# Sample attention of a hybrid decoder step: score matmuls by halves of the keys, rope part in eight tiles of the array

## The reference

```python
def _mla_scores(q_lat, q_rope, lat, krope):
    s = jnp.einsum('bhqc,bkc->bhqk', q_lat, lat) + jnp.einsum('bhqr,bkr->bhqk', q_rope, krope)
    return s.astype(jnp.float32) * MLA_SCALE

def _softmax_accumulate(carry, s, vals):
    m, l, acc = carry
    m_new = jnp.maximum(m, jnp.max(s, axis=-1))
    corr = jnp.exp(m - m_new)
    p = jnp.exp(s - m_new[..., None])
    l_new = l * corr + jnp.sum(p, axis=-1)
    acc_new = acc * corr[..., None] + jnp.einsum('bhqk,bkc->bhqc', p, vals.astype(jnp.float32))
    return (m_new, l_new, acc_new)

    def page_step(carry, pt):          # pt: one page (128 keys) of each sequence
        lat = lat_pool[e, pt]
        kr = rope_pool[e, pt]
        s = _mla_scores(q_lat, q_rope, lat, kr)
        return _softmax_accumulate(carry, s, lat), None
```

## Time and profile before

| | |
|---|---|
| time of three runs, median | 1405.76 us (1404.13 to 1409.06) |
| the profiled execution | 1405.4 us |
| its span | 1403.5 us |
| TensorE busy in the span | 1377.5 us, 98% |
| VectorE, ScalarE, GpSimd busy | 803.4, 582.3, 113.3 us |
| granted clock of TensorE, mean | 0.996 of full speed |
| sample attention, from its first score matmul to step 0 of the output projection | 531.7 to 607.3 us |

### The profile page before, as it was taken

How to read it: one execution, slowest core, us unless ns; L and a number is a source line. 1 busy time by engine, 2 the same in 40 slices (tenths; PEclk the granted TensorE clock), 3 DMA queues, 4 the chain that set the end, 5 groups by cost and what they waited for, 6 DMA issues and landing times.

```text
span 1403.5 us, 24497 instructions
## 1 busy us (share of the span) xinstructions
PE 1377.5 (98%) x9830; PEld 1228.1 (88%) x9830; DVE 803.4 (57%) x1509; ACT 582.3 (41%) x1044; POOL 113.3 (8%) x213
## 2 busy tenths in 40 slices
PE   9999999999999999999999999999999999999996
PEld 9988999767667666689998888999999999999996
DVE  4486843174575665655886344324445659545676
ACT  4169522146556565533553233214553125212343
POOL 1000000000000305700002000010000010000000
PEclk9999999999999999999999999999999999999998
DMA  6211032220001127855556211124334030114562
GB/s 213 63 30 46 31 123 90 84 92 14 1 1 44 33 71 218 239 178 164 187 194 235 74 62 31 61 62 70 67 61 114 31 106 31 47 64 149 169 213 104
DMA packets 59298, 135.75 MB, mean 97 GB/s; under 512 B 9001, under 2 KB 37898, under 8 KB 58418
## 3 DMA queue, kind: packets, MB, share of 16 engines
q1 hardware_dynamic: 48882, 112.45, 24.4%
q0 software_dynamic: 10160, 21.56, 6.5%
q10 hardware_dynamic: 144, 0.18, 0.0%
HBM read 120.65 MB, written 13.50 MB: 96 GB/s over the span
## 4 chain that ended last, share of the span: by engine, by line
PE 86%; DVE 6%; SPq 3%; issue 2%; ACT 2%; DMA 0%; DVEq 0%; ACTq 0%
PE ps L553 14%; PE ps L555 14%; PE ps L554 14%; PE ps L682 5%; PE ps L684 5%; PE ps L683 5%; PE ps L1094 3%; PE ps L1106 2%; PE ps L1135 2%; SPq L2766 2%; PE ps L1264 2%; PE ps L3089 1%; PE ps L566 1%; PE ps L3098 1%; PE ps L3093 1%
## 5 line engine op out<-in xcount | busy, mean ns | idle before, releaser
L553 PE MATMUL ps<-x_hi,w_hi 128*128 128x352 f32 x1288 | 425.6, 330 | 0.0
L555 PE MATMUL ps<-x_hi,w_lo 128*128 128x352 f32 x1288 | 414.7, 322 | 0.0
L554 PE MATMUL ps<-x_lo,w_hi 128*128 128x352 f32 x1288 | 414.0, 321 | 0.0
L553 PEld LDWEIGHTS ps<-x_hi,w_hi 128*128 128x128 f32 x1288 | 242.3, 188 | 10.0 <-issue 9.5
L554 PEld LDWEIGHTS ps<-x_lo,w_hi 128*128 128x128 f32 x1288 | 243.1, 189 | 1.3 <-issue 1.0
L555 PEld LDWEIGHTS ps<-x_hi,w_lo 128*128 128x128 f32 x1288 | 242.2, 188 | 0.0
L495 ACT ACTIVATE w_hi<-w_raw 128x1024 fp32r<-128x1024 f32 (+1 forms) x105 | 121.2, 1154 | 246.9 <-PE ps L555 136.3
L501 DVE TENSOR_TENSOR w_lo<-w_raw,w_hi 128x1024 fp32r<-128x1024 f32 (+1 forms) x105 | 141.1, 1344 | 63.5 <-ACT w_hi L495 63.0
L682 PE MATMUL ps<-mx_hi,w_hi 128*128 128x352 f32 x480 | 157.7, 328 | 0.3 <-issue 0.2
L684 PE MATMUL ps<-mx_hi,w_lo 128*128 128x352 f32 x480 | 154.1, 321 | 0.0
L683 PE MATMUL ps<-mx_lo,w_hi 128*128 128x352 f32 x480 | 153.9, 321 | 0.0
(11 more groups left out here) (490 smaller groups left out, 1950.5 us busy)
## 6 DMA issues: line engine op xcount, KB each, us to landing
w_raw<-in_w_out SPq DMA_DIRECT2D x48, 640.0 KB, 3.9
w_raw<-in_w_in SPq DMA_DIRECT2D x57, 512.0 KB, 3.6
page<-in_cache_mla SPq DMA_DIRECT2D x128, 128.0 KB, 2.5
kvs<-in_mem_cache SPq DMA_DIRECT2D x16, 512.0 KB, 5.2
x_res<-in_xT SPq DMA_DIRECT2D x24, 176.0 KB, 2.4
x<-x_next POOLq DMA_DIRECT2D x3, 1408.0 KB, 7.6
x_res<-x SPq DMA_DIRECT2D x24, 176.0 KB, 2.3
w_mem<-in_w_mem SPq DMA_DIRECT2D x2, 2048.0 KB, 10.4
```

The lines of the kernel that those rows point to most:

```text
L553: pe.matmul(out, w_hi[:, (u + 1) % 2, kk], x_hi[:, k, chunk(c)], start=(k == 0), stop=False)
L554: pe.matmul(out, w_hi[:, (u + 1) % 2, kk], x_lo[:, k, chunk(c)], start=False, stop=False)
L555: mm = pe.matmul(out, w_lo[:, (u + 1) % 2, kk], x_hi[:, k, chunk(c)], start=False, stop=(k == KX - 1))
```

## The change

1. The scores of a round lie in two banks, 0 and 1: the first half of the 512 keys (`pair` 0, 256 keys) in bank 0 and the second half (`pair` 1) in bank 1. Even rounds use columns 0 to 255 of both banks, and odd rounds columns 256 to 511. Before, a round had one bank.
2. The latent part has 16 matmuls over 256 keys in place of 8 over 512.
3. The rope part has 8 matmuls over 256 keys in place of 4 over 512. They stand in eight different tiles of 32 by 32: sequence j keeps its column strip, and the row strip is `2 * (j // 2) + pair`. The rope keys are loaded to match: two sequences share a row strip, side by side in columns. The number and size of the loads stay.
4. The maximum and the exponential read the two halves as one operand with two pieces of 256.
5. `scores(5)`, the short round of group 1, moves from before the turn of round 6 to behind `transposes(4)`.
6. The steps of layer 0's output projection use bank `(n + 2) % 6`, so that the first of them leave banks 0 and 1 alone while round 9 is read. `BANK_FREE` follows: tile (31, 0) waits for step 22 in place of 18, (31, 1) for step 23 in place of 19, (31, 2) for 18 in place of 20, and tile 32 for steps 19, 20, 21 in place of 21, 22, 23.

The core of the diff:

```diff
+        def rope_rows(j, pair):
+            r = 32 * (2 * (j // 2) + pair)
+            return slice(r, r + 32)
+        def rope_cols(j):
+            return PAIR_COLS * (j % 2)
...
                 for k in range(2):
+                    for pair in range(2):
+                        for j in range(4):
+                            pe.matmul(ps[32 * j:32 * j + 32, pair, a:a + PAIR_COLS], rows_of(qs[:, k], g, j),
+                                      latT[:, j, k, PAIR_COLS * pair:PAIR_COLS * pair + PAIR_COLS],
+                                      start=(k == 0), stop=False, skip_group_check=True)
+                for pair in range(2):
                     for j in range(4):
-                        pe.matmul(ps[32 * j:32 * j + 32, e % 2, :], rows_of(qs[:, k], g, j), latT[:, j, k, :],
-                                  start=(k == 0), stop=False, skip_group_check=True)
-                for j in range(4):
-                    rr = slice(32 * j, 32 * j + 32)
-                    mm = pe.matmul(ps[rr, e % 2, :], rows_of(qsr[rr], g, j), ropeT[real(e) % 3][rr, :], start=False, stop=True,
-                                   skip_group_check=True)
+                        rr, cc = rope_rows(j, pair), rope_cols(j)
+                        mm = pe.matmul(ps[32 * j:32 * j + 32, pair, a:a + PAIR_COLS], rows_of(qsr[rr], g, j),
+                                       ropeT[real(e) % 3][rr, cc:cc + PAIR_COLS], start=False, stop=True,
+                                       skip_group_check=True)
...
-                    v.then(dve.tensor_reduce(col(2), bank(e % 2), AX_X, ALU.max))
+                    v.then(dve.tensor_reduce(col(2), pairs_of(e), AX_XY, ALU.max))
...
-            out = bank(n % 6, n=CH)
+            out = bank(step_bank(l, n), n=CH)
```

More of the change, by code:

```diff
@@ L27 @@
 AX_X = mybir.AxisListType.X
+AX_XY = mybir.AxisListType.XY
 P = 128
@@ L588, in build @@
             k for k in SLOTS_IN0 + SLOTS_IN1 if TILES[k[0]].kind in SIGMOIDS)}
-        BANK_FREE = {(31, 0): ZI[(0, *STEPS[18])], (31, 1): ZI[(0, *STEPS[19])], (31, 2): ZI[(0, *STEPS[20])],
-                     (32, 0): ZI[(0, *STEPS[21])], (32, 1): ZI[(0, *STEPS[22])], (32, 2): ZI[(0, *STEPS[23])]}
+        BANK_FREE = {(31, 0): ZI[(0, *STEPS[22])], (31, 1): ZI[(0, *STEPS[23])], (31, 2): ZI[(0, *STEPS[18])],
+                     (32, 0): ZI[(0, *STEPS[19])], (32, 1): ZI[(0, *STEPS[20])], (32, 2): ZI[(0, *STEPS[21])]}
         BANK_FREE.update({(33, c): ZI[(31, c)] for c in range(NCH)})
@@ L664, in sp_residual, with step_bank @@
             sp.dma_start(x_res[:, n % 2, :], src).then_inc(xr_in[n % 2], 16)
+        def step_bank(l, n):
+            return (n + (2 if l == 0 else 0)) % 6
         def pe_step(pe, l, n):
@@ L690, in dve_step @@
             dve.wait_ge(xr_in[n % 2], 16 * (12 * l + n // 2 + 1))
-            dve.scalar_tensor_tensor(res[:, t, chunk(c)], x_res[:, n % 2, :], ALPHA, bank(n % 6, n=CH),
+            dve.scalar_tensor_tensor(res[:, t, chunk(c)], x_res[:, n % 2, :], ALPHA, bank(step_bank(l, n), n=CH),
                                      ALU.mult, ALU.add).then_inc(z_free, 1)
@@ L1751, in col, with pairs_of @@
             return stat[:, c:c + 1]
+        PAIR_COLS = 2 * P
+        def pairs_of(e):
+            return ps[:, 0:2, PAIR_COLS * (e % 2):PAIR_COLS * (e % 2) + PAIR_COLS]
+        def rope_rows(j, pair):
[3 more added lines that the diff above has]
+            return PAIR_COLS * (j % 2)
         UNIT_BANKS = (2, 3, 6, 7)
@@ L1795, in scores @@
                     pe.wait_ge(ss_p, e - 1)
+                a = PAIR_COLS * (e % 2)
                 if i < 0:
@@ L1798, in scores @@
                         for j in range(4):
-                            out = ps[32 * j:32 * j + 32, e % 2, 0:SM]
+                            out = ps[32 * j:32 * j + 32, 0, a:a + SM]
                             if k < 2:
@@ L1886, in rest @@
                     nxt = e + 1 if e != 4 else 6
+                    turn(nxt, range(1 if e == 0 else 0, 6))
+                    transposes(e)
                     if e == 4:
                         scores(5)
-                    turn(nxt, range(1 if e == 0 else 0, 6))
-                    transposes(e)
                     turn(nxt, range(6, 8))
@@ L1925, in exps @@
                                                 bias=col(COL_NB + e % 2), scale=MLA_SCALE))
-                out = sp_self[:, :] if i < 0 else sp_p[:, e % 2, :]
-                act.activation(out, ps[:, e % 2, 0:out.shape[1]], ACT.Exp, bias=col(COL_NB + e % 2),
+                if i < 0:
+                    out, src = sp_self[:, :], pairs_of(e)[:, 0, 0:SM]
+                else:
+                    out, src = sp_p[:, e % 2, :].rearrange("p (b c) -> p b c", b=2), pairs_of(e)
+                act.activation(out, src, ACT.Exp, bias=col(COL_NB + e % 2),
                                scale=MLA_SCALE, accum_out=col(COL_S + e % 2)).then_inc(ss_p, 1)
@@ L1988, in maxima @@
                 if i < 0:
-                    s = ps[:, e % 2, 0:SM]
+                    s = pairs_of(e)[:, 0, 0:SM]
                     v.then(dve.tensor_tensor(s, s, selfmask[:, g, :], ALU.add))
@@ L2850, in _ @@
                     for q in range(4):
-                        gp.dma_start(ropeT[r % 3][32 * j:32 * j + 32, q * P:q * P + P],
+                        c = rope_cols(j) + (q % 2) * P
+                        gp.dma_start(ropeT[r % 3][rope_rows(j, q // 2), c:c + P],
                                      x["cache_rope"][bass.ds(four[q], 1), :, :].rearrange(
```

## The result

The changed kernel took 1408.38 us (median of 9 runs, 1405.53 to 1411.76) beside 1406.06 us for the kernel before on the same chip (9 runs). The ratio is 1.0022 [1.0013, 1.003]. Forecast were 1405.0 us and a range up to 1407.5. So the time went the other way than forecast, and lies above the range. The profiled execution is one of the faster ones: 1405.95 us, with a span of 1404.4 us against 1403.5 before. A second look at the same kernel (experiment 2) had a span of 1408.4.

What follows compares the result with a forecast made beforehand. TensorE was taken as the bound, except between 548 and 600 us, where SyncE's page loads pace it. Two savings of 0.40 us off the 1405.76 median gave 1405.0 us; range 1403.4 to 1406.4, 8 in 10 1402.6 to 1407.5.

Steps and rivals of the forecast that it cites:

- Rope part: Rope matmuls of a round's scores: eight tiles run together, 0.57 us instead of 1.00, saving 0.43.
- Two tiles at a time: Rival, slower: rope matmuls run in four sets, 1.85 us a round, giving 1407.5 us in all; chance 0.06.
- Latent part: Latent matmuls of a round's scores: 32 records of 256 columns cost 0.03 us more than the 1.83 before.
- A round: TensorE's scores of one round with pages: 0.43 saved less 0.03 lost, 0.40 us, in eight rounds.
- Start of the run of loads: First round's scores release SyncE's queue earlier, so its page loads and the last landing move 0.40 us forward.
- Round 9: Its scores stand after the last page's landing, directly before step 0, so their 0.40 us saving counts.
- Reads by halves: Maximum and exponential reading two pieces of 256 instead of one of 512: costed at nothing.
- scores(5): Moving this short round within the stretch covered by loads: no cost; 0.15 us without that cover.
- banks of the steps: Rotated output-step banks cost nothing: tile (31, 0) has 1.75 us to spare, (31, 1) 10.5.
- SyncE's run of 80 loads starts at about 547.7 and is as long as before: SyncE's page loads of rounds 3 to 7: start earlier than 548.08, unchanged length, covering the six rounds between.
- the −0.80 at step 0: Total saving on the path before step 0: 0.40 us from earlier loads plus 0.40 from the last round's scores.
- TensorE's idle time before the last page: TensorE's wait for the last page grows from 1.12 to some 3 us, as six covered rounds save 2.4.

Runs made afterwards that it cites:

- experiment 2: The changed kernel timed again with no edit: 1407.96 us, ratio 1.0015 to the kernel before.
- experiments 5 and 6: 120 already satisfied waits added early on TensorE, to the kernel before (1407.97 us, ratio 1.0013) and to the changed kernel (1405.82 us, 1.0001).
- experiment 8: Changed kernel with SyncE reading the page numbers of rounds 3 to 5 before its wait for TensorE: 1405.42 us, ratio 0.9995.
- experiment 9: Changed kernel with 20 page loads moved from SyncE's to ScalarE's queue, from r = 3 on: 1401.33 us, ratio 0.9971.

## Why the prediction was wrong, point by point

- **Rope part:** forecast 0.57 us, measured 0.59. Eight tiles run together. Two tiles at a time would have made it 1.85. The bank rule of the Trainium skill's TensorEngine Tiling, section Restrictions and Gotchas, would lead there, and the trace does not agree. By the Trainium skill's TensorE: Matmul & The Clock Gate, section Part 3: Packing small matmuls, an estimate is 0.60, and the trace agrees.
- **Latent part:** forecast 1.86, measured 1.84. **A round:** forecast 0.40 less, measured 8.66 − 8.26 = 0.40.
- **Start of the run of loads:** forecast 547.7, measured 547.75. **Round 9:** from the last page's landing to step 0 it takes 608.27 − 601.76 = 6.51 instead of 607.29 − 600.38 = 6.91 us. Both places on the path gave what they were to give.
- **Reads by halves, scores(5), banks of the steps:** forecast nothing. The reduction takes 692 ns as before, the exponential 670 ns against 671, `scores(5)` 0.46 us against 0.45, and (31, 0) and the steps keep their distance from step 0.
- **"SyncE's run of 80 loads starts at about 547.7 and is as long as before":** this step failed. The run grew by 1.73 us in the profile and by 3.65 in the second look. That turns the −0.80 at step 0 into +0.98 and +2.29. The prediction counted TensorE's 48 further instructions of a round only as streaming. It treated the run of issues as a fixed cover, and named a change of its length as what would make the forecast wrong, without a price for it. That term was put at nothing without a reason, and measured +1.73. The rows gave a hint, 0.61 us for a load in the earlier trace rows against 0.33 for an issue in the earlier trace rows, but a weak one: most of the difference is the spacing of the issues, 0.52, and the four gaps, and only 2.04 / 80 = 0.03 us of it is hanging.
- **TensorE's idle time before the last page:** forecast some 3 us, measured 1.18. The savings of the covered rounds were spent earlier, at four other waits for pages, 5.0 us in all.
- **The rest of the +2.3 us** between the medians is put down to the clock, by an estimate. The changed kernel's executions have a mean clock of 0.9939 and 0.9945 against 0.9955, worth 2.2 and 1.4 us. A bare copy of before had 0.9947, so part of that is chance. No clocks are recorded for the executions of the kernel before that stood beside the first nine; 0.9955 is from the later ones.

What stays open. That the fetch makes the issue hang is shown by the ends of the 49 issues and by experiments 5 and 6, which move the one and thereby the other. What in the chip joins the two is not shown, nor why a packet of 16 KB is under way for 0.88 us at one place and 1.89 at another. The reads by halves and the moved `scores(5)` had no experiment of their own; in the trace their operations take as long as before. Not shown either is where the slower executions of the changed kernel lose their clock. A drop behind an idle time, like that of experiment 8, could be it, since these idle times reach 1.70 and 2.31 us against 1.12 before. That was only argued: neither profile of this kernel has one there.

## What to carry to other kernels

Before a saving on the engine that looks like the bound is counted, see whether a queue of issues paces it. Here, with 20 of the 128 page loads on another queue, the change gave 0.23%, of which 0.14% is in the stretch; with all on one queue it cost 0.22%. When an edit adds instructions to a long unrolled stream, count them as moving every later instruction fetch too. Before a difference of 0.1 to 0.2% is credited to an edit, run both versions with a few satisfied waits added early. If the sign changes, as here, placement decides and not what the edit computes.

## What the runs showed of the hardware

- An issue of a page load on SyncE takes 0.33 us. It took up to 1.79 us when a 16 KB packet of instructions for TensorE came in (1.61 in the changed kernel, 1.38 in the one before). Each of the 49 issues that began right behind another one within such a packet ended 0.22 to 0.39 us behind the packet's end; the first issue behind a gap passed in 14 of 15 cases. 120 added waits on TensorE moved a run of 80 issues by +3.04 and by −1.14 us.
- Reading sixteen page numbers takes a queue 1.5 us in which it issues nothing. Two such gaps less shortened the run of issues even with more hanging.
- Eight tiles of 32 by 32, two in each row strip and column strip, each with its own moving data and two banks in all, streamed 256 fp32 columns in 0.59 us.
- The granted clock drops to half, the 1.2 GHz level, once near 1112 us, for 3.4 or 6.8 us, with no edit nearby and TensorE busy for all of 1100 to 1130 us. Over 1100 to 1130 us it is 0.94 of full speed in six of the fourteen profiles, 0.89 in seven and 1.00 in one (experiment 9). A step of that is 1.5 to 1.8 us of the span. Spans of single profiles are therefore compared over the stretch and not as a whole.
